# One kernel, seven small edits: who splits two weight pieces, how the first squares are summed, RG-LRU's ScalarE order, and value products ahead of the turning in block two

## The reference

```python
# block one, layer 1: dilated attention, 3 groups x 8 heads; layer 2: RG-LRU; each followed by a conv FFN
x = x + rms_norm(dilated_attention(rms_norm(x, g), w_qkv, w_o, rel_bias), g_post)
x = x + rms_norm(conv_ffn(rms_norm(x, g)), g_post)

def rglru(x):                       # layer 2
    h = x @ w_in; xb, gb = halves(h); gate = gelu(gb)
    xb = causal_dwconv(xb)
    r = sigmoid(block_diag(xb, ga_w) + ga_b); i = sigmoid(block_diag(xb, gx_w) + gx_b)
    log_a = 8 * r * log_sigmoid(lam); a = exp(log_a)
    b = sqrt(-expm1(2 * log_a)) * i * xb
    return (scan(a, b) * gate) @ w_out

# block two, two layers of
z = rmsnorm(x, g) @ w_in            # q, k, v, gates of three branches
o_a = compressed + selected + window attention   # 8 heads of 64
o_b = forgetting attention                       # 8 heads of 64
o_m = attention to 256 memory rows               # 4 heads of 128
x = x + (sum of gated o_a @ w_a, o_b @ w_b, o_m @ w_m) @ w_out
```

## Time and the profile before

| | us |
|---|---|
| median of three timed runs | 3042.14 |
| the three runs | 3040.51 to 3047.27 |
| span of the profiled execution | 3050.7 |
| the profiled execution's own time | 3052.15 |
| PE busy | 2998.7 (98% of the span) |
| POOL, DVE, ACT busy | 1936.4, 1483.3, 803.5 |

### The profile page before, as it was taken

One profiled execution on the slowest core, in us unless ns is written; L12 is line 12 of the kernel. 1 busy time (PEld: TensorE's weight loads), 2 busy tenths in 40 slices (PEclk: granted clock), 3 DMA queues, 4 the chain that ended last, 5 costly groups with the idle time before them and its releaser, 6 DMA issues.

```text
span 3050.7 us, 41907 instructions
## 1 busy us (share of the span) xinstructions
PE 2998.7 (98%) x15546; PEld 2516.8 (82%) x15554; DVE 1483.3 (49%) x3007; ACT 803.5 (26%) x1751; POOL 1936.4 (63%) x2202
## 2 busy tenths in 40 slices
PE   9999999999999989999999999999999999999999
PEld 8888888888888878888888887888888887888887
DVE  1333334377740593877304746663233463664332
ACT  1111111232210342222103225662102213664110
POOL 5555555589987797999876762125777484222775
PEclk8999999999999999999999999999999899999999
DMA  4222222123232222222323231112333232111222
GB/s 142 102 88 90 92 92 86 62 79 98 97 100 97 76 83 70 97 97 97 116 97 126 90 97 43 29 36 70 97 115 114 85 109 70 36 43 34 91 97 90
DMA packets 70217, 261.48 MB, mean 86 GB/s; under 512 B 8320, under 2 KB 8832, under 8 KB 68224
## 3 DMA queue, kind: packets, MB, share of 16 engines
q1 hardware_dynamic: 65696, 232.81, 23.5%
q10 hardware_dynamic: 4320, 25.99, 2.3%
HBM read 251.43 MB, written 2.10 MB: 83 GB/s over the span
## 4 chain that ended last, share of the span: by engine, by line
PE 92%; DVE 3%; issue 2%; POOL 2%; ACT 1%; DMA 0%; ACTq 0%; POOLq 0%; DVEq 0%
PE bank L370 24%; PE bank L371 24%; PE bank L372 24%; PE bank L1895 3%; PE bank L1880 2%; PE bank L410 2%; PE bank L397 1%; PE bank L662 1%; PE bank L402 1%; PE bank L398 1%; PE bank L1861 1%; POOL w_lo L2247 1%; PE bank L1598 1%; PE bank L1306 1%; PE bank L634 1%
## 5 line engine op out<-in xcount | busy, mean ns | idle before, releaser
L2247 POOL TENSOR_TENSOR w_lo<-w_raw,w_hi 128x256 fp32r<-128x256 f32 x1736 | 1403.8, 839 | 36.2
L2243 POOL TENSOR_SCALAR w_hi<-w_raw 128x1024 fp32r<-128x1024 f32 x434 | 489.9, 1129 | 1047.3 <-PE bank L372 932.0
L370 PE MATMUL bank<-in_hi,w_hi 128*128 128x512 f32 x1408 | 555.3, 394 | 0.8 <-POOL w_lo L2247 0.5
L372 PE MATMUL bank<-in_hi,w_lo 128*128 128x512 f32 x1408 | 549.1, 390 | 0.0
L371 PE MATMUL bank<-in_lo,w_hi 128*128 128x512 f32 x1408 | 548.5, 390 | 0.0
L370 PE MATMUL bank<-z_hi,w_hi 128*128 128x512 f32 x976 | 392.4, 402 | 0.0
L372 PE MATMUL bank<-z_hi,w_lo 128*128 128x512 f32 x976 | 381.4, 391 | 0.0
L371 PE MATMUL bank<-z_lo,w_hi 128*128 128x512 f32 x976 | 380.8, 390 | 0.0
L372 PEld LDWEIGHTS bank<-in_hi,w_lo 128*128 128x128 f32 x1408 | 264.7, 188 | 56.1
L370 PEld LDWEIGHTS bank<-in_hi,w_hi 128*128 128x128 f32 x1408 | 264.9, 188 | 54.0 <-issue 0.9
L371 PEld LDWEIGHTS bank<-in_lo,w_hi 128*128 128x128 f32 x1408 | 265.0, 188 | 52.4
(11 more groups left out here) (436 smaller groups left out, 5103.0 us busy)
## 6 DMA issues: line engine op xcount, KB each, us to landing
w_raw<-in_units SPq DMA_DIRECT2D x434, 512.0 KB, 3.5
bias<-in_bias ACTq DMA_DIRECT2D x8, 1152.0 KB, 5.1
o_all<-in_cmp_w ACTq DMA_DIRECT2D x4, 2048.0 KB, 8.1
x_res<-in_x ACTq DMA_DIRECT2D x4, 512.0 KB, 9.1
mem_in<-in_mem ACTq DMA_DIRECT2D x2, 1024.0 KB, 8.6
nsa_q_hi<-nsa_q_hi SPq DMA_DIRECT2D x16, 128.0 KB, 2.3
nsa_q_lo<-nsa_q_lo SPq DMA_DIRECT2D x16, 128.0 KB, 2.3
out<-x_res ACTq DMA_DIRECT2D x4, 512.0 KB, 2.6
```

Source lines behind the costliest of these rows:

```text
L370: pe.matmul(out, hi[:, w], rh, start=start and n == 0, stop=False)
L372: last = pe.matmul(out, lo[:, w], rh, start=False, stop=stop and n == len(tiles) - 1)
L2243: d = c.s.unit_hi.on(pool.tensor_scalar(c.w_hi[s][:, :], c.w_raw[s][:, :], 1.0, 0.0, ALU.mult, ALU.add))
L2247: last = pool.tensor_tensor(c.w_lo[s][:, w], c.w_raw[s][:, w], c.w_hi[s][:, w].bitcast(F32), ALU.subtract)
```

## The change

Seven parts, none of which changes what is computed:

1. The squares of the norm `attn` and of block two's second layer stay in eight buffers; DVE adds squares 1 to 6 into square 0, and PE sums twice (the total and square 7) instead of eight times.
2. `pe_norm_spread` of `attn` stands before the fourth unit instead of behind it; the wait for the identity moves there from the program's start. The warm matmuls go from 40 to 30 at the start and from 16 to 8 at the end of the attention.
3. Two units, the second of the program and the fourth of the attention's output product, are split by ACT (`w_hi`, one 128x1024 copy) and DVE (`w_lo`, one 128x1024 subtraction). SP's load of unit 2 waits for the second part of x. ACT starts the loads of lru, taps and bias after the norm's chunks.
4. RG-LRU: ACT's decays stand elsewhere among convolutions and gates, square roots 0 to 3 come before gates 3; DVE does scans 0 and 1 before roots 6 and 7.
5. Block two's attention: `pe_output` before `pe_turn` in each step.
6. The product of the compressed values stands one slot later, on PE and ACT.
7. The widening of the last slot is done with that of the slot before.

```diff
-    def __init__(self, name, src, gain, hi, lo, sq, r, n_tiles=TT, banks=(7, 6), heads=False):
+    def __init__(self, name, src, gain, hi, lo, sq, r, n_tiles=TT, banks=(7, 6), heads=False, added=False):
...
+BY_OTHERS = (("qkv", 1), ("attn_out", 3))
+def split_done(c, u):
+    return (c.s.piece_split if c.order[u] in BY_OTHERS else c.s.unit_split)[u]
+def act_split(act, c, key):
+    u = c.order.index(key)
+    act.wait_ge(*c.s.unit_loaded[u % SLOTS][u])
+    if u >= SLOTS:
+        act.wait_ge(*c.s.unit_multiplied[u - SLOTS])
+    c.s.piece_hi.on(act.activation(c.w_hi[u % SLOTS][:, :], c.w_raw[u % SLOTS][:, :], ACT.Copy), u)
+def dve_split(dve, c, key):
+    u = c.order.index(key)
+    s = u % SLOTS
+    dve.wait_ge(*c.s.piece_hi[u])
+    c.s.piece_split.on(dve.tensor_tensor(c.w_lo[s][:, :], c.w_raw[s][:, :], c.w_hi[s][:, :].bitcast(F32), ALU.subtract), u)
...
 def pe_norm_sum(pe, c, z, k):
+    if z.added and k < DC - 1:
+        return
+    b = c.bank[z.banks[0]]
+    if z.added:
+        pe.wait_ge(*c.s.squares_added[z.name, DC - 2])
+        pe_sum_tokens(pe, c, b, z.square(0), z.n_tiles, True, False, (z.name, 0))
...
     pe_project(pe, c, keys[2], c.bank[2][:, :], z.hi, z.lo)
+    pe_norm_spread(pe, c, z)
     if len(keys) == 4:
         pe_project(pe, c, keys[3], c.bank[3][:, :], z.hi, z.lo)
-    pe_norm_spread(pe, c, z)
...
-    pe_warm(pe, c, 4, 16)
+    pe_warm(pe, c, 4, 8)
...
+    if z.added and 0 < k < DC - 1:
+        total = z.square(0)[:, 0:z.n]
+        dve.wait_ge(*c.s.squared[z.name, k])
+        if k > 1:
+            dve.wait_ge(*c.s.squares_added[z.name, k - 1])
+        c.s.squares_added.on(dve.tensor_tensor(total, total, z.square(k)[:, 0:z.n], ALU.add), (z.name, k))
...
         if n in (4, 6):
             act_lru_gates(act, c, n // 2 - 2)
-            act_lru_decay(act, c, n - 4)
-            act_lru_decay(act, c, n - 3)
+        if n == 5:
+            act_lru_decay(act, c, 0)
+            act_lru_decay(act, c, 1)
+    act_lru_decay(act, c, 2)
     act_lru_parts(act, c, DC - 1)
+    act_lru_decay(act, c, 3)
     act_lru_gates(act, c, 2)
     act_lru_decay(act, c, 4)
     act_lru_decay(act, c, 5)
+    for ch in range(4):
+        act_lru_sqrt(act, c, ch)
     act_lru_gates(act, c, 3)
...
+    dve_lru_scan(dve, c, 0)
+    dve_lru_scan(dve, c, 1)
     dve_lru_root(dve, c, 6)
...
-            if what == "spread" and s.heads == 2:
+            if what == "spread" and s.heads == 2 and m < SLOTS_TWO:
                 act_widen(act, c, layer, s)
+                if m == SLOTS_TWO - 1:
+                    act_widen(act, c, layer, every[SPREAD[SLOTS_TWO]])
...
     yield from pe_compress(pe, c, layer, 1)
+    yield
...
+        if 0 <= now - 4 < TASKS:
+            pe_output(pe, c, tasks[now - 4])
         if 0 <= now - 2 < TASKS:
             pe_turn(pe, c, tasks[now - 2])
-        if 0 <= now - 4 < TASKS:
-            pe_output(pe, c, tasks[now - 4])
...
-    pe_warm(pe, c, 4, 40)
-    pe.wait_ge(*c.s.ident_loaded["all"])
+    pe_warm(pe, c, 4, 30)
```

More of the change, by code:

```diff
@@ L87, in __init__ @@
         self.halves_moved = new("halves_moved")
+        self.piece_hi, self.piece_split = new("piece_hi_by_act"), new("piece_split_by_vector")
         self.unit_hi, self.unit_split, self.post_added = new("unit_hi_done"), new("unit_split"), new("post_added")
@@ L160 @@
 class Norm:
-    def __init__(self, name, src, gain, hi, lo, sq, r, n_tiles=TT, banks=(7, 6), heads=False):
+    def __init__(self, name, src, gain, hi, lo, sq, r, n_tiles=TT, banks=(7, 6), heads=False, added=False):
+        self.added = added
         self.name, self.src, self.gain, self.hi, self.lo, self.sq, self.r = name, src, gain, hi, lo, sq, r
@@ L166, in __init__, with square @@
         self.wide = r.wide[:, 0:n_tiles * P]
+    def square(self, k):
+        n = len(self.sq)
+        return self.sq[k % n if not self.added or not k else 1 + (k - 1) % (n - 1)]
     def head_factor(self, heads):
@@ L318, in norms @@
         return {
-            "attn": Norm("attn", self.x, self.gain(0, 0), self.hi, self.lo, self.sq, self.r),
+            "attn": Norm("attn", self.x, self.gain(0, 0), self.hi, self.lo, [self.y[:, k, :] for k in range(DC)], self.r, added=True),
             "ffn0": Norm("ffn0", self.x, self.gain(2, 0), self.hi, self.lo, self.cg, self.r),
@@ L325, in layer_norm @@
     def layer_norm(self, layer):
-        return Norm(("z", layer), self.x, self.cols[:, layer, C_NORM:C_NORM + DC], self.zh, self.zl, self.z_sq, self.zr, heads=True)
+        return Norm(("z", layer), self.x, self.cols[:, layer, C_NORM:C_NORM + DC], self.zh, self.zl, self.z_sq, self.zr, heads=True, added=layer == 1)
     def memory_norm(self, layer):
@@ L365, in pe_unit @@
     hi, lo = c.w_hi[c.u % SLOTS], c.w_lo[c.u % SLOTS]
-    pe.wait_ge(*c.s.unit_split[c.u])
+    pe.wait_ge(*split_done(c, c.u))
     for out, tiles, start, stop in jobs:
@@ L395, in pe_together @@
             if k == 0:
-                pe.wait_ge(*c.s.unit_split[first + u])
+                pe.wait_ge(*split_done(c, first + u))
             pe.matmul(out, c.w_hi[(first + u) % SLOTS][:, w], hi[:, k, :], start=k == 0, stop=False)
@@ L420, in pe_norm_sum @@
 def pe_norm_sum(pe, c, z, k):
+    if z.added and k < DC - 1:
[4 more added lines that the diff above has]
+        pe_sum_tokens(pe, c, b, z.square(0), z.n_tiles, True, False, (z.name, 0))
     pe.wait_ge(*c.s.squared[z.name, k])
-    pe_sum_tokens(pe, c, c.bank[z.banks[0]], z.sq[k % len(z.sq)], z.n_tiles, k == 0, k == DC - 1, (z.name, k))
+    pe_sum_tokens(pe, c, b, z.square(k), z.n_tiles, k == 0, k == DC - 1, (z.name, k))
 def pe_norm_spread(pe, c, z):
+    if z.name == "attn":
+        pe.wait_ge(*c.s.ident_loaded["all"])
     pe.wait_ge(*c.s.factor_found[z.name])
@@ L476, in act_norm_chunk @@
     c.s.hi_done.on(act.activation(z.hi[:, k, :], z.src[:, k, :], ACT.Copy, scale=z.gain[:, k:k + 1]), (z.name, k))
-    if k >= len(z.sq):
+    if z.added and k >= len(z.sq):
+        act.wait_ge(*c.s.squares_added[z.name, k - len(z.sq) + 1])
+    elif k >= len(z.sq):
         act.wait_ge(*c.s.tokens_summed[z.name, k - len(z.sq)])
-    c.s.squared.on(act.activation(z.sq[k % len(z.sq)][:, 0:z.n], z.src[:, k, :], ACT.Square), (z.name, k))
+    c.s.squared.on(act.activation(z.square(k)[:, 0:z.n], z.src[:, k, :], ACT.Square), (z.name, k))
 def act_norm_wide(act, c, z):
@@ L739, in act_attention_one @@
             act.wait_ge(*c.s.biased[h - 2, DIL - 1])
+        if h == 0:
+            act_norm_start(act, c, z, lambda k: c.s.x_loaded[k // 2]["all"])
+            c.s.lru_loaded.on(act.dma_start(c.lru[:, :], c.t["lru"]), "all", 16)
+            c.s.taps_loaded.on(act.dma_start(c.taps[:, :], c.t["taps"]), "all", 16)
         c.s.bias_loaded[h % 2].on(act.dma_start(c.bias[h % 2][:, :], c.t["bias"][h]), h, 16)
         for j in range(9):
-            if h == 0 and j == 0:
-                act_norm_start(act, c, z, lambda k: c.s.x_loaded[k // 2]["all"])
             if h == HEADS - 1 and j == 0:
@@ L1052, in act_lru_decay, with act_lru_sqrt @@
     c.s.act_step.on(act.activation(c.lru_t[ch % 2][:, :], c.ga[:, ch, :], ACT.Square), ("decay", ch))
+def act_lru_sqrt(act, c, ch):
+    act.wait_ge(*c.s.dve_step["root", ch])
+    c.s.act_step.on(act.activation(c.th[:, ch, :], c.th[:, ch, :], ACT.Sqrt), ("sqrt", ch))
 def act_lru_gelu(act, c, ch):
@@ L1082, in act_lru @@
     act_lru_decay(act, c, 7)
-    for ch in range(DC):
-        act.wait_ge(*c.s.dve_step["root", ch])
-        c.s.act_step.on(act.activation(c.th[:, ch, :], c.th[:, ch, :], ACT.Sqrt), ("sqrt", ch))
+    for ch in range(4, DC):
+        act_lru_sqrt(act, c, ch)
     for ch in range(5):
@@ L1169, in dve_lru @@
     for ch in range(DC):
-        dve_lru_scan(dve, c, ch)
+        if ch >= 2:
+            dve_lru_scan(dve, c, ch)
         if ch in (1, 3, 5):
@@ L2202, in act_program @@
     c.s.ident_loaded.on(act.dma_start(c.ident[:, :], t["ident"]), "all", 16)
-    c.s.lru_loaded.on(act.dma_start(c.lru[:, :], t["lru"]), "all", 16)
-    c.s.taps_loaded.on(act.dma_start(c.taps[:, :], t["taps"]), "all", 16)
     act.wait_ge(*c.s.gains_loaded["all"])
+    act_split(act, c, ("qkv", 1))
     act_attention_one(act, c, norms["attn"])
+    act_split(act, c, ("attn_out", 3))
     act_out(act, c, "attn_out", [("attn_out", n) for n in range(DC)], (0, 1, 2, 3))
@@ L2222, in dve_program @@
     dve.wait_ge(*c.s.gains_loaded["all"])
+    dve_split(dve, c, ("qkv", 1))
     dve_attention_one(dve, c, norms["attn"])
+    dve_split(dve, c, ("attn_out", 3))
     dve_out(dve, c, "attn_out")
@@ L2239, in pool_program @@
         s = u % SLOTS
+        if c.order[u] in BY_OTHERS:
+            continue
         pool.wait_ge(*c.s.unit_loaded[s][u])
@@ L2291, in sp_program @@
         if u >= SLOTS:
-            sp.wait_ge(*c.s.unit_split[u - SLOTS])
+            sp.wait_ge(*split_done(c, u - SLOTS))
+        if u == 2:
+            sp.wait_ge(*c.s.x_loaded[1]["all"])
```

## The result

| | before | changed |
|---|---|---|
| median of the timed runs, us | 3044.48 (four runs, 3040.51 to 3047.27) | 3021.89 (four runs, 3021.76 to 3022.05) |
| profiled execution: time, span, us | 3052.15, 3050.7 | 3021.99, 3020.5 |

The ratio is 0.9927, with a 95% interval of 0.991 to 0.9944: 22.6 us faster. Forecast were 2997, 45 us less than the 3042.14 known then, with a range of 2982 to 3017; the result lies outside. The direction held, the size was half.

What follows compares the result with a forecast made beforehand. PE, busy 98% of the span, was taken as the bound. Terms A to H summed to −42.4 us, −44.1 with B's dip; with a microsecond for half clock, −45 from 3042.14 gave 2997, range 2982 to 3017.

Steps and rivals of the forecast that it cites:

- G: Block two's attention: value products ahead of the turn cover PE's waits for the probabilities; −10 us, range −4 to −13.
- Rival 3: Slower kernel: value products ahead of the turn wait for ACT's copy, losing 96d over some 96 wide steps; chance 0.03.
- D: RG-LRU: the 1.2 us wait before gates 2 and a third of the `w_lo` wait go; −3 us, range +2 to −9.
- F: Block two: the turns no longer wait 2 × 1.2 us for the widened part, made before; −2.4 us.
- C: End of block one's attention: eight warm matmuls fewer and no wait for POOL's remainder; −2.3 us, range −1.5 to −2.9.
- H: Block two's second layer: eight sets of sums of squares become two; −5 us, range −4 to −5.6.
- rival 1: Start stays at half clock, third unit near 32.5 instead of 24, gain 6.5 instead of 14, about 3005; chance 0.22.
- B: Spread before the fourth unit: waits for `vt` vanish; −1.75 us, 1.7 more if the dip goes; range 0 to −3.5.
- A: Program's start: third unit begins at about 24 instead of 39.12 us; −14 us taken.
- Rival 5: DVE's additions delay POOL where PE waits for it, only at the start, 3 to 6 us, about 3001; chance 0.08.
- the prediction's 14: By the skill's SBUF exclusion rule, twelve DVE additions and two subtractions would hold POOL for some 14 us.
- E: Block two: the product of compressed values, one slot later, no longer waits 2 × 1.96 us for DVE; −3.9 us.

Runs made afterwards that it cites:

- e1: Changed kernel with the turn before the value product again in block two's attention; 3011.54 us against 3021.89.
- e2: Kernel before with only the value product put before the turn; 3047.83 us against 3042.19, ratio 1.0013.
- e3: Changed kernel with VectorE's store of a task's product one step earlier in block two's attention; 3006.39 us, ratio to before 0.9875.
- e10: e3 with the turn before the value product again, so the early store alone; 3010.00 us.
- e11: Kernel before with 47 warm matmuls at the start instead of 40; 3038.85 us against 3044.63, ratio 0.9986.
- e4: Changed kernel with PE summing the squares of the norm `attn` behind every piece again, eight times instead of two; 3025.98 us.
- e7: e3 with GpSimd splitting the fourth unit of the attention's output product again and 16 warm matmuls instead of 8; 3004.79 us.
- e6: e3 with RG-LRU's order on ScalarE and VectorE as before the change; 3008.64 us.
- e5: e3 with ScalarE instead of GpSimd making `w_hi` of the first two units of RG-LRU's output product; 3002.79 us against 3006.39.
- e9: e5 with ScalarE making `w_hi` of four units in RG-LRU, two of the gelu branch added; 2999.21 us, ratio to before 0.9851.
- e8: e3 with block two's second layer summing the square of every piece on PE again; 3012.36 us.

## Why the prediction failed, and where it held

**The step that failed is G.** It said −10, range −4 to −13; it measured +6.3. I had paired each wait at the turn with the value product behind it, and asked of the product only whether ScalarE's copy of the turned probabilities was there. The product also needs its PSUM bank, and I named no queue for it. Rival 3 had the right form (the value products wait once they are ahead) with the wrong releaser: it looked for `at_pt`, for which 0.4 us are waited, and so found 0.07 us of slack and a chance of 0.03. The store of the task two back on VectorE was in the code, and its place in VectorE's step would have shown it. e1, e2, e3 and e10 show this from four sides. Even with the bank free, 7.5 us are gained and not 10.9 to 13.0: value products still wait 3.6 us for `o_rows` (2.6 for the compressed keys, 1.0 in the forgetting attention), and 3.5 us stay at the turn, where the product ahead of it is shorter than the wait. Waits of PE fell by 9.9 us from before to e3 at these lines; where the other 2.4 went was not looked for.

That is 16.3 of the 22.4 us that are missing. D and F, below, are 2.5 more. **The rest, some 4 to 5 us, is the clock** (C and H gave 0.9 more than forecast). The runs of the kernel before differ by 14.6 us (3037.35 to 3051.98) with granted clocks from 0.998 down to 0.992, and all four of the changed kernel show 0.997. In the profile 6.9 us of it are the 14 us near 1626. The two medians are therefore not at one clock. With the shares of the clock taken off (a run at clock c loses about 3020 × (1−c); c is given to 0.001, so this is good to 1.5 us), the thirteen runs of before beside e1 come to about 3030 and the changed kernel to 3012.8: some 17 us of work and gaps, and some 5 of clock, where the forecast held some 10 of clock (7.5 at the start, the distance to rival 1, 1.7 for the dip of B and a microsecond). It held no dip for the changed kernel. What makes one near 1626 in this kernel, near 2370 in the one before and at neither place in e1's profile (two of e1's other runs show 0.997) was not found; no experiment aimed at it.

**A, the start: right.** The third unit begins at 25.42, forecast about 24 (−14 taken, −13.7 measured). The clock stays at 1.00, so rival 1 (0.22) did not come; e11 and e4 split the gain: filling the gap and the clock 6.6, fewer sums 4.1, the rest the earlier start. Rival 1 read the start of before wrongly as paced by ScalarE's wait: PE was busy for all of 12.00 us, and ScalarE's squares waited for PE's sums (6.3 us ahead of the one at 17.87). Two of my readings were off. ScalarE's table load waited for the unit's transfer and came at 7.54, not 5.41, so the second unit's remainder was ready at 11.2 (8.4 to 10.5 forecast), and the first piece began at 10.55, not 9.6. ScalarE's first rows in the changed kernel:

```profile
7.54 1.28 ACT L382 ACT_TABLE_LOAD   x1 [7.54 <-DMA w_raw<-in_units]
8.83 1.06 ACT L382 ACTIVATE w_hi<-w_raw 128x1024 fp32r<-128x1024 f32 x1
```

And VectorE's `lo` and addition took 1.3 us a chunk alone and 2.3 where GpSimd worked beside them:

```profile
13.06 0.75 DVE L529 SCALAR_TENSOR_TENSOR in_lo<-x_res,gains,in_hi 128x512 fp32r<-128x512 f32 x1
13.73 0.68 DVE L536 TENSOR_TENSOR out_y<-out_y 128x512 f32<-128x512 f32 x1
...
18.20 1.23 DVE L529 SCALAR_TENSOR_TENSOR in_lo<-x_res,gains,in_hi 128x512 fp32r<-128x512 f32 x1
19.35 1.22 DVE L536 TENSOR_TENSOR out_y<-out_y 128x512 f32<-128x512 f32 x1
```

GpSimd's four instructions for one `w_lo` took 4.49 us beside them and 2.77 alone. That is the contention which the Trainium skill describes in "SBUF — State Buffer", "Who interferes with whom", and the trace agrees that VectorE's two-input instructions and GpSimd's hold each other up. Rival 5 named it; PE felt it at the start as two waits for `in_lo`, 1.0 us in all (the other 1.9 of the 2.9 stand elsewhere, and 1.8 stood there before), and not as a late GpSimd. In the whole span GpSimd was busy 1939.0 us, 2.6 more than before, though it splits two units less (2 × 3.8 us alone): an estimate from these gives some 10 us of holding, of the order of the prediction's 14.

**B: right.** The dip in 50 to 58 and both waits went; up to the same matmul near 59 us PE was 17.4 us ahead, against 17.5 forecast for A and B with the dip.

**C: right.** 2.63 us (e7), forecast 2.3. The copy took 1.06 and the subtraction 1.23 to 1.32, inside their bounds.

**D: half.** −3 forecast; 1.4 measured by e6, and 3.7 in the two profiles, dips included. What was said of it held: 4.8 of the 5.3 us remained, because no GpSimd instruction had been removed; e5 and e9 removed some, and the wait fell to 2.5 and 0.7 (with 1.0 for ScalarE).

**E, F: right for E** (the waits for `cmp_hidden` are gone, some 4 us); **F gave 1.5 instead of 2.4**, as the same turns now wait 0.9 for `fox_q`.

**H: right.** 5.6 us (e8), forecast 5, upper bound 5.6: a piece without sums is 0.93 us shorter (2.29 − 1.36), not 0.81, as allowed for.

So seven of eight terms (−32.4 forecast, with B's dip −34.1) came out within 2 us each, and one had the wrong sign.

## What to carry to other kernels

When a product is moved ahead in an engine's order, list every semaphore it waits for, its output bank's too, and for each find where the releaser stands in its own engine's step: the wait that the old order covered is the one that appears. Such a move is often half of an edit; here the other half was one store on VectorE a step earlier, and only both gained. A busy engine off the critical path (GpSimd in RG-LRU) is relieved by taking instructions off it, not by reordering its neighbours.

## What the runs showed of the hardware

Seven more matmuls that compute nothing (1.0 us, 12.32 instead of 11.34 for all of them) shortened a gap of PE from 2.1 to 0.9 us, and 12 us of the start ran at 1.00 where they had run at 0.50. And a kernel's runs can differ by 0.5% through the granted clock alone (3037.35 at 0.998, 3051.98 at 0.993), with stretches of 14 us at 0.50 that fall at another place or not at all in a variant that differs elsewhere, and the one near 1626 came after 36 us in which PE was busy without a gap. In RG-LRU the half clock followed a wait: 6.8 us of it behind a wait of 4.8 us in e3 (3.4 in the changed kernel), 3.4 behind 2.5 in e5, none behind waits of 1.0 and 0.7 in e9. Terms of a few us were therefore read at their place in the trace, and not from the time.
